# Attention of a hybrid decoder layer: the repetition of the inverse softmax denominators moves from VectorE to ScalarE

## The chip, the cores and the metric

The kernel runs on one core of one Trainium2 chip. The metric is the device time of one execution in microseconds. Three runs of the kernel before stand beside one execution that the hardware profiler recorded; the times of the profile count from the start of its span.

## What is computed

The reference is one step of a decoder layer for a prompt of 512 tokens and for 8 sample tokens that share the weights. Cut to what matters here:

```
z  = rms_norm(x) @ w_in            # q, k, v of 12 heads x 64; B, C, u of the short convolution
q, k = rope(rms_norm(heads))       # per head
m = max(s);  p = exp(s - m);  den = sum(p);  num = p @ v       # per dilated window (128,1), (512,4), (2048,16)
attn = sum(num_i * c_i) / sum(den_i * c_i)                     # the three windows merged
y  = B * conv3_causal(C * u)
h  = x + concat(rms_norm(attn), rms_norm(y)) @ w_out
out = h + top-2-of-8-experts(in the best of 4 groups, rms_norm(h))   # 32 gated MLPs of 1024 x 256
```

For the prompt, the kernel merges the three windows by adding the logarithm of how many windows hold a key to the score, so that one softmax per head does. The division by the denominator is what the change touches.

## The kernel before

The program is written by hand for each engine; each engine runs its own list in order and waits on semaphores. Stages: input projection and rotary norm (to about 178 us of the span), prompt attention with the short convolution between (178 to 254 us), output projection, routing and the choice of experts (254 to 341 us), and the 32 experts in 16 pairs, whose weights stream through three slots of `ring`.

The prompt's attention has 24 units, `pair_units`: query tile `qt` from 3 down to 0, and in each the six head pairs `hp`. A unit has n = (qt + 1) x 128 keys, so its width falls from 512 to 128 columns. The stage is a software pipeline over `p` from 0: each engine's list holds, in iteration p, a piece of several units.

- PE in iteration p: the scores of unit p (L816), the transposition of the exponentials of unit p - 1 (L933, into `turn_bank`), and for u = p - 2 the product of the probabilities with v (L949) and behind it one transposition of `rden_b` (L952), which raises `o_done`.
- DVE in iteration p: `masked_scores` of unit p (L1695: adds `logc`, keeps the minimum of the negated scores), for u = p - 1 the reciprocal of two denominators (L1759), the copy of the second head's transposed exponentials out of PSUM (L1760), and the repetition of the two inverses over 64 columns each into `rden_b` (L1762), which raises `p_evac_v`; then a piece of the convolution (`convolve`, p = 2 to 11); last, for u = p - 3, the product of the result in PSUM with the turned inverses (L1777, by the helper of L1521), which raises `o_evac`.
- ACT in iteration p: the exponentials of unit p for both heads (L1377, with the sum of the row by an accumulator read), for u = p - 3 the copy of the turned inverses out of PSUM into `rden_t` (L1384), for u = p - 1 the copy of the first head's transposed exponentials (L1394). In iteration 12 a square of the convolution's result follows (L1397), in iteration 16 the squares of the sample rows (L1402).
- POOL, once `w_out` has landed (210 us): for every unit one scaling of 512 columns of `w_out` (L2267, 16 times), and the square (L2273) and the running sum (L2274) of the attention's result.

A head's inverse denominator stands on the partition of its query, the result of L949 on the partition of its channel. So the inverse is repeated over 64 columns, turned by PE into a tile with the queries along the columns, and multiplied in. PE waits for `p_evac_v` ahead of L949 and for nothing ahead of L952.

## Time and profile before

| | |
|---|---|
| median of three runs | 596.61 us (594.55 to 598.19) |
| profiled execution, its own time | 592.48 us |
| its span | 590.7 us |
| PE, DVE, ACT, POOL busy | 545.4, 274.7, 167.9, 155.4 us |
| granted TensorE clock, mean | 0.983 |
| prompt attention on PE | about 178 to 254 us |

Busy time is the time in which an engine has an instruction in work. PE's matmuls overlap and their ends are modelled, so idle time of PE in a stretch is only what no modelled matmul covers. "idle before" of a group is the idle time of its engine just ahead of its instructions, with what ended it. DVE's L1521 is the line of a helper for products of two tensors; its tiles tell which one it is (`ring<-bank,ring` 128x128 is the product with the turned inverses, `work<-work,ring` 128x512 a product of the convolution).

### The profile page before, as it was taken

The page shows a single profiled execution, that of the slowest core. Times are in us where ns is not written, and L with a number is a line of the kernel's source. Part 1 is how long each engine was busy: PE and PEld are TensorE (multiplying, and loading weights), DVE is VectorE, ACT ScalarE, POOL GpSimd, SP SyncE. Part 2 cuts the span into 40 slices and gives each one's busy share as a digit, 9 for nine tenths or more (in the row PEclk, how much of TensorE's full clock was granted, in tenths as well). Part 3 has the DMA queues.
Part 4 walks back from the last instruction along what each step waited for, and adds up shares of the span by engine and source line. Part 5 has one row for each costly group of instructions (what it writes and reads, how often), then busy time and mean ns, then how long its engine had stood idle before and what let it go on. Part 6 is the DMA issues. An engine that isn't in the chain of part 4 may idle for free.

```text
span 590.7 us, 8412 instructions
## 1 busy us (share of the span) xinstructions
PE 545.4 (92%) x2970; PEld 318.3 (54%) x2970; DVE 274.7 (47%) x695; ACT 167.9 (28%) x386; POOL 155.4 (26%) x187
## 2 busy tenths in 40 slices
PE   6899999999999999999999999999996969689994
PEld 4798799897765665554555944333332323234321
DVE  5887686978403998723458631111210111111235
ACT  7445343413411566631412320101100100000013
POOL 0488788510001079610000021211210111100003
PEclk9999999999999999999999999999997979999998
DMA  7991333489774950039914869999999999999956
GB/s 280 281 272 51 123 134 94 152 249 301 238 196 150 381 208 2 3 95 383 413 41 173 327 194 414 418 421 420 421 420 422 421 419 421 419 422 418 378 235 260
DMA packets 48215, 163.48 MB, mean 277 GB/s; under 512 B 8674, under 2 KB 22058, under 8 KB 36888
## 3 DMA queue, kind: packets, MB, share of 16 engines
q1 hardware_dynamic: 41360, 144.93, 64.9%
q0 software_dynamic: 6528, 17.01, 8.1%
q10 hardware_dynamic: 288, 1.05, 0.4%
q8 instruction: 21, 0.34, 0.2%
q14 instruction: 18, 0.15, 0.1%
HBM read 151.06 MB, written 19.76 MB: 289 GB/s over the span
## 4 chain that ended last, share of the span: by engine, by line
PE 49%; DMA 17%; SPq 11%; DVE 5%; POOL 3%; issue 3%; ACT 2%; DVEq 0%; POOLq 0%; ACTq 0%
PE bank L1144 10%; DMA ring<-in_w_up_dram 10%; PE bank L1068 9%; SPq L540 7%; PE bank L1171 4%; DMA x<-q_rows 3%; SPq L553 3%; PE bank L816 2%; PE bank L933 2%; DMA ring<-results 2%; PE bank L949 2%; PE bank L838 2%; POOL ring L2225 2%; PE bank L1019 2%; PE bank L839 2%
## 5 line engine op out<-in xcount | busy, mean ns | idle before, releaser
L1144 PE MATMUL bank<-ring,work 128*64 128x512 f32 x512 | 120.1, 624 | 16.9 <-DMA ring<-in_w_up_dram 16.9
L1144 PEld LDWEIGHTS bank<-ring,work 128*64 128x64 f32 x512 | 39.1, 143 | 94.5 <-issue 80.5
L1521 DVE TENSOR_TENSOR work<-work,bank 128x256 f32<-128x256 f32 x16 | 6.7, 422 | 132.5 <-ACT work L1456 132.5
L759 PE MATMUL bank<-split 128*128 128x384 f32 x192 | 66.1, 344 | 0.7 <-DVE split L1521 0.7
L1171 PE MATMUL bank<-ring,work 128*64 128x512 f32 x256 | 58.5, 598 | 7.6 <-ACT work L1460 7.6
L760 PE MATMUL bank<-split 128*128 128x384 f32 x192 | 64.3, 335 | 0.0
L1068 PE MATMUL bank<-ring 128*128 128x512 f32 x96 | 42.9, 596 | 0.0
L1456 ACT ACTIVATE work<-bank 128x256 f32<-128x256 f32 x16 | 6.1, 384 | 128.5 <-PE bank L1144 128.5
L2292 POOL DMA_INDIRECT work<-hn_rows,tbl x15 | 15.2, 1016 | 101.7 <-PE bank L1154 89.7
L2300 POOL DMA_INDIRECT results<-work,tbl x15 | 15.0, 1001 | 99.1 <-DVE work L2070 99.1
L2225 POOL TENSOR_TENSOR ring<-ring 128x192 f32<-128x192 f32 (+1 forms) x40 | 38.8, 989 | 8.0 <-DVEq L1616 6.8
L1521 DVE TENSOR_TENSOR split<-ring,split 128x768 fp32r<-128x768 f32 (+1 forms) x35 | 37.3, 1099 | 6.1 <-PE bank L746 5.8
L790 PE MATMUL bank<-split 128*128 128x384 f32 x192 | 37.8, 337 | 0.5 <-DVE split L1521 0.5
L759 PEld LDWEIGHTS bank<-split 128*128 128x128 f32 x192 | 36.1, 188 | 3.5 <-issue 1.3
L1171 PEld LDWEIGHTS bank<-ring,work 128*64 128x64 f32 x256 | 17.0, 136 | 38.8 <-issue 27.4
L1377 ACT ACTIVATE ring<-ring,st 128x512 f32<-128x512 f32 (+3 forms) x48 | 26.6, 554 | 35.3 <-DVE st L1695 35.3
L760 PEld LDWEIGHTS bank<-split 128*128 128x128 f32 x192 | 36.1, 188 | 0.0
L2070 DVE COPY work<-bank 128x512 f32<-128x512 f32 x15 | 10.4, 692 | 52.8 <-PE bank L1171 52.8
L790 PEld LDWEIGHTS bank<-split 128*128 128x128 f32 x192 | 33.4, 188 | 1.7 <-DVE split L1521 1.0
L1068 PEld LDWEIGHTS bank<-ring 128*128 128x128 f32 x96 | 17.8, 190 | 20.1 <-issue 20.1
L1256 ACT ACTIVATE split<-ring 128x768 fp32r<-128x768 f32 x32 | 25.1, 833 | 3.8 <-DMA ring<-in_w_in_dram 3.8
L1469 ACT ACTIVATE work<-bank 128x512 f32<-128x512 f32 x15 | 9.0, 597 | 57.1 <-PE bank L1171 57.1
(281 smaller groups left out, 865.1 us busy)
## 6 DMA issues: line engine op xcount, KB each, us to landing
ring<-in_w_down_dram SPq DMA_DIRECT2D x32, 1024.0 KB, 24.7
ring<-in_w_gate_dram SPq DMA_DIRECT2D x28, 1024.0 KB, 23.1
ring<-in_w_up_dram SPq DMA_DIRECT2D x28, 1024.0 KB, 24.9
ring<-in_w_in_dram SPq DMA_DIRECT2D x7, 1536.0 KB, 11.7
results<-work POOLq DMA_DIRECT2D x1, 4160.0 KB, 24.7
x<-in_x_prompt_dram SPq DMA_DIRECT2D x8, 512.0 KB, 15.5
ring<-in_w_out_dram SPq DMA_DIRECT2D x2, 2048.0 KB
ring<-in_w_gate_dram SPq DMA_DIRECT2D x8, 512.0 KB, 13.2
```

The lines of the kernel that those rows point to most:

```text
L540: sp.dma_start(gate_up[s][h][:, o, :, :], w[0, ds(e, 1)].rearrange("e (p k) f -> p (e k) f", p=P)).then_inc(gu_in[s], 16)
L553: sp.dma_start(down[s][h], w_down[0, ds(e, 1)].rearrange("e (p k) n -> p (e k) n", p=P)).then_inc(dn_in[s], 16)
L759: pe.matmul(bank[n % 3][:, 0:CW], xT_high[:, k, cols], w_high[c][:, k, :], start=(k == 0), stop=False)
L760: pe.matmul(bank[n % 3][:, 0:CW], xT_low[:, k, cols], w_high[c][:, k, :], start=False, stop=False)
L790: last = pe.matmul(bank[n % 3][:, 0:CW], xT_high[:, k, cols], w_low[c][:, k, :], start=False, stop=(k == KD - 1))
L1068: last = pe.matmul(bank[g][:, :], src, wout[g % 2][:, k, :], start=(k == rng[0]), stop=(k == rng[-1]))
L1144: last = pe.matmul(bank[2][64 * h:64 * h + 64, :], xgT[:, k, 64 * h:64 * h + 64], gate_up[s][h][:, :, k, :], start=(k == 0), stop=(k == KD ...
L1171: last = pe.matmul(bank[4 + j][64 * h:64 * h + 64, :], hT[:, c, 64 * h:64 * h + 64], down[s][h][:, c, j * 512:(j + 1) * 512], start=(c == ...
L1256: act.activation(w_high[c][:, 2 * i:2 * i + 2, :], wchunk[c][:, 2 * i:2 * i + 2, :], ACT.Copy)\
L1377: act.activation(buf, buf, ACT.Exp, bias=nmax[:, u % 4:u % 4 + 1], scale=-1.0, accum_out=den[:, u % 24:u % 24 + 1]).then_inc(S["exp_done"], 1)
L1521: return dve.tensor_tensor(out, a, b, op)
L2225: last = pool.tensor_tensor(sv[:, :, a * half:(a + 1) * half], zv[:, :, b * half:(b + 1) * half], bc(rope_g[2 * (cc // 2) + 1][0:w, t, a * ...
```

## The change

DVE writes the two inverses and raises a new semaphore `inverted`; the copy of the exponentials behind it raises `p_evac_v`. ACT waits for `inverted` behind its own copy of the exponentials, repeats the two inverses over 64 columns into `rden_b`, and raises `rden_wide`. PE waits for `rden_wide` between L949 and the transposition of `rden_b`. Three semaphores that were each raised once (`gains_turned`, `a_turned`, `conv_turned`) become the three counts of one, `rows_turned`.

```diff
@@ PE
-            pe.transpose(bank[7][:, 0:30], ...).then_inc(S["gains_turned"], 1)
+            pe.transpose(bank[7][:, 0:30], ...).then_inc(S["rows_turned"], 1)
...
-                last.then_inc(S["conv_turned"], 1)
+                last.then_inc(S["rows_turned"], 1)
...
-                last.then_inc(S["a_turned"], 1)
+                last.then_inc(S["rows_turned"], 1)
...
                             pe.matmul(bank[6 + u % 2][h * DH:(h + 1) * DH, 0:P],
                                       v_rows[:, j, (2 * hp + h) * DH:(2 * hp + h + 1) * DH],
                                       probs_t[u % 2][h][:, j * P:(j + 1) * P], start=(j == 0), stop=(j == qt))
+                    pe.wait_ge(S["rden_wide"], u + 1)
                     pe.transpose(bank[6 + u % 2][:, P:2 * P], rden_b[:, u % 2, :, :].rearrange("p h d -> p (h d)"), ident[:, :])\
                         .then_inc(S["o_done"], 1)
@@ ACT
                     act.activation(probs_t[u % 2][0][:, 0:n], turn_bank[0][:, 0:n], ACT.Copy).then_inc(S["p_evac_a"], 1)
+                    act.wait_ge(S["inverted"], u + 1)
+                    act.activation(rden_b[:, u % 2, :, :], bc(rden[:, u % 2, :], 2, DH, [P, 2, DH]), ACT.Copy)\
+                        .then_inc(S["rden_wide"], 1)
                 if p == 12:
...
-            act.wait_ge(S["conv_turned"], 1)
+            act.wait_ge(S["rows_turned"], 3)
@@ DVE
                     if u >= 2:
                         dve.wait_ge(S["o_done"], u - 1)
-                    inverse = chain.put(dve.reciprocal(rden[:, u % 2, :], den[:, (2 * u) % 24:(2 * u) % 24 + 2]))
-                    dve.tensor_copy(probs_t[u % 2][1][:, 0:n], turn_bank[1][:, 0:n])
-                    chain.need(inverse)
-                    dve.tensor_copy(rden_b[:, u % 2, :, :], bc(rden[:, u % 2, :], 2, DH, [P, 2, DH])).then_inc(S["p_evac_v"], 1)
+                    dve.reciprocal(rden[:, u % 2, :], den[:, (2 * u) % 24:(2 * u) % 24 + 2]).then_inc(S["inverted"], 1)
+                    dve.tensor_copy(probs_t[u % 2][1][:, 0:n], turn_bank[1][:, 0:n]).then_inc(S["p_evac_v"], 1)
...
-                    dve.wait_ge(S["a_turned"], 1)
+                    dve.wait_ge(S["rows_turned"], 2)
```

How the lists stand at two places. The lines of the changed kernel count from its own text: L1385 is L1384 of before, L1395 is L1394, L1406 is L1402, L1378 is L1377, L1763, L1764 and L1525 are L1759, L1760 and L1521, and L1397 is the new copy on ACT.

ACT in iteration 16, where the squares of the sample rows stand; before:

```order
L1384 ACTIVATE ring<-bank 128x128 [waits o_evac,o_done]
L1394 ACTIVATE ring<-bank 128x256 [waits o_done,p_turned]
L1402 ACTIVATE work,st<-ring 8x768 [waits rows_out]
L1377 ACTIVATE ring,st<-ring,st 128x256 [waits masked] x2
L1384 ACTIVATE ring<-bank 128x128 [waits o_evac,o_done]
```

and with the change:

```order
L1385 ACTIVATE ring<-bank 128x128 [waits o_evac,o_done]
L1395 ACTIVATE ring<-bank 128x256 [waits o_done,p_turned]
L1397 ACTIVATE ring<-ring 128x128 [waits inverted]
L1406 ACTIVATE work,st<-ring 8x768 [waits rows_out]
L1378 ACTIVATE ring,st<-ring,st 128x256 [waits masked] x2
L1385 ACTIVATE ring<-bank 128x128 [waits o_evac,o_done]
```

The new copy stands behind the copy of the exponentials and ahead of the squares and of the next unit's exponentials; so it does in each of the 24 units.

DVE in iteration 10, where the last products of the convolution stand; before:

```order
L1759 RECIPROCAL ring<-st 128x2 [waits o_done,p_turned]
L1760 COPY ring<-bank 128x384
L1762 COPY ring<-ring 128x128 [waits dve_link]
L1521 TENSOR_TENSOR work<-work,ring 128x512
L1521 TENSOR_TENSOR ring<-bank,ring 128x128 [waits p_evac_a,o_done]
L1695 ISA ring,st<-bank,rt 128x384 [waits p_turned,s_done]
```

and with the change:

```order
L1763 RECIPROCAL ring<-st 128x2 [waits o_done,p_turned]
L1764 COPY ring<-bank 128x384
L1525 TENSOR_TENSOR work<-work,ring 128x512
L1525 TENSOR_TENSOR ring<-bank,ring 128x128 [waits p_evac_a,o_done]
L1699 ISA ring,st<-bank,rt 128x384 [waits p_turned,s_done]
```

The repetition is gone from between the copy of the exponentials and the products. (In iteration 8 the same piece of the list stands, for the other half of the channels.) On PE nothing changes place; the transposition L952, now L953, has a wait of its own.

## Rows read from the trace of the kernel before

**Rows 1.** The page: busy time of the engines, and the chain that ended last.

```profile
PE 545.4 (92%) x2970; PEld 318.3 (54%) x2970; DVE 274.7 (47%) x695; ACT 167.9 (28%) x386; POOL 155.4 (26%) x187
...
PE 49%; DMA 17%; SPq 11%; DVE 5%; POOL 3%; issue 3%; ACT 2%; DVEq 0%; POOLq 0%; ACTq 0%
```

**Rows 2.** Busy time by stretches: length, engines (instructions), granted clock, DMA share, GB/s.

```profile
188.00:220.00 32.00, 31.87 (x268) 19.41 (x262) 28.86 (x95) 18.43 (x53) 10.48 (x16) 1.00 0.85 319
220.00:236.00 16.00, 14.59 (x129) 9.14 (x125) 13.86 (x54) 11.14 (x40) 14.82 (x24) 1.00 0.01 3
236.00:254.00 18.00, 16.93 (x139) 8.97 (x139) 11.72 (x63) 11.89 (x53) 12.19 (x23) 1.00 0.01 2
254.00:330.00 76.00, 75.76 (x306) 41.49 (x305) 36.91 (x155) 20.87 (x33) 2.94 (x5) 1.00 0.64 241
```

**Rows 3.** Start of the experts' weights on SyncE, and a piece of the chain (start, length, what).

```profile
260.38 0.41 SPq L572 DMA_DIRECT2D ring<-in_w_gate_dram  x1
...
419.03 29.77 DMA ring<-in_w_up_dram
```

**Rows 4.** DVE's repetition as a group, and its shortest, median and longest.

```profile
L1762 DVE COPY ring<-ring 128x128 f32<-128x128 f32 x24 | 9.6, 401 | 0.0
...
L1762 DVE COPY ring<-ring x24: 210/220/1094, 191.8 to 251.3; 128x128 f32<-128x128 f32 x24
```

**Rows 5.** Timeline of iterations 10 and 11: DVE, POOL and PE (start, length).

```profile
220.43 1.09 DVE L1762 COPY ring<-ring 128x128 f32<-128x128 f32 x1
221.44 1.25 DVE L1521 TENSOR_TENSOR work<-work,ring 128x512 f32<-128x512 f32 x2
222.61 0.28 DVE L1521 TENSOR_TENSOR ring<-bank,ring 128x128 f32<-128x128 f32 x1
...
220.40 1.04 POOL L2267 TENSOR_TENSOR ring<-ring,gains 128x512 f32<-128x512 f32 x1
...
222.94 0.88 PE L949 MATMUL bank<-ring 128*64 128x128 f32 x12 [0.52 <-DVE ring L1521]
...
225.38 0.30 PE L933 MATMUL bank<-ident,ring 128*128 128x128 f32 x1 [0.67 <-ACT ring L1394]
```

**Rows 6.** Timeline of iteration 8: a product of the convolution beside POOL's sum.

```profile
215.31 0.68 DVE L1521 TENSOR_TENSOR work<-work,ring 128x512 f32<-128x512 f32 x1
215.91 0.28 DVE L1521 TENSOR_TENSOR ring<-bank,ring 128x128 f32<-128x128 f32 x1
...
215.38 0.92 POOL L2274 TENSOR_TENSOR ring<-ring 128x128 f32<-128x128 f32 x1
```

**Rows 7.** Timeline of ACT around iteration 12, with its square of 1040 columns.

```profile
227.79 1.06 ACT L1397 ACTIVATE ring<-work 128x1040 f32<-128x1040 f32 x1
228.75 0.50 ACT L1377 ACTIVATE ring<-ring,st 128x256 f32<-128x256 f32 x1
...
229.73 0.26 ACT L1384 ACTIVATE ring<-bank 128x128 f32<-128x128 f32 x1
229.89 0.38 ACT L1394 ACTIVATE ring<-bank 128x256 f32<-128x256 f32 x1
```

**Rows 8.** Timeline of ACT and PE around iterations 16 and 17.

```profile
236.56 0.83 ACT L1402 ACTIVATE work<-ring 8x768 f32<-8x768 f32 x1
...
239.09 0.63 PE L933 MATMUL bank<-ident,ring 128*128 128x128 f32 x4 [0.39 <-ACT ring L1394]
```

**Rows 9.** Timeline of one unit of 128 keys on ACT, and PE's transposition of the inverses.

```profile
243.98 0.26 ACT L1394 ACTIVATE ring<-bank 128x128 f32<-128x128 f32 x1
...
244.71 0.40 ACT L1377 ACTIVATE ring<-ring,st 128x128 f32<-128x128 f32 x1 [0.47 <-DVE st L1695]
...
245.11 0.33 PE L952 MATMUL bank<-ident,ring 128*128 128x128 f32 x1
```

**Rows 10.** Groups of ACT in the stage, shapes apart: exponentials, 128 and 256 columns.

```profile
L1377 ACT ACTIVATE ring<-ring,st 128x256 f32<-128x256 f32 x12 | 6.0, 501 | 2.8 <-DVE st L1695 2.8
...
L1377 ACT ACTIVATE ring<-ring,st 128x128 f32<-128x128 f32 x12 | 4.7, 393 | 3.1 <-DVE st L1695 3.1
```

More of the change, by code:

```diff
@@ L302, in build @@
         names = """const_in gains_in misc_in x_evac_p wr_in wout_in logc_in
-            row_std x_scaled x_turned x_whole x_high x_evac w_high_done w_low_done gains_turned rope_ready pads_zero
+            row_std x_scaled x_turned x_whole x_high x_evac w_high_done w_low_done rows_turned rope_ready pads_zero
             z_done z_squared z_ssq z_std z_copied z_normed z_cos z_sin z_summed rot_turned rot_evac v_evac rows_out
-            part_done part_evac comb_done comb_read gates_turned gates_read blk_done blk_evac_a blk_evac_v cu_ready conv_done y_squared pool_made ssc_done
-            ssc_std conv_std state_turned conv_turned conv_evac conv_out
+            part_done part_evac comb_done comb_read gates_turned gates_read blk_done blk_evac_a blk_evac_v cu_ready conv_done y_squared inverted rden_wide pool_made ssc_done
+            ssc_std conv_std state_turned conv_evac conv_out
             q_out scores_s turned_s soft_in soft_done probs_turned probs_placed v_used pv_s head_done
@@ L309, in build @@
             s_done masked exp_done p_turned p_evac_a p_evac_v o_done o_evac
-            a_squared a_std a_turned a_evac opp_done op_done op_evac opp_evac h_done
+            a_squared a_std a_evac opp_done op_done op_evac opp_evac h_done
             h_root h_scaled h_turned h_evac r_done r_evac
@@ L644, in _ @@
             pe.wait_ge(S["gains_in"], 80)
-            pe.transpose(bank[7][:, 0:30], gain_in[0:30, :], ident[0:30, 0:30]).then_inc(S["gains_turned"], 1)
+            pe.transpose(bank[7][:, 0:30], gain_in[0:30, :], ident[0:30, 0:30]).then_inc(S["rows_turned"], 1)
             def keep_warm(n, where):
@@ L1528, in _ @@
             dve.wait_ge(S["pads_zero"], 1)
-            dve.wait_ge(S["gains_turned"], 1)
+            dve.wait_ge(S["rows_turned"], 1)
             chain.step(dve.tensor_copy(gains[:, 0:30], bank[7][:, 0:30]))
```

## The prediction

> **What bounds the kernel now.** I read the page first for who bounds the whole [rows 1]: PE is busy for 92% of the span and holds 49% of the chain that ended last; DVE is busy for 47% and holds 5%. So an edit on DVE or ACT pays only where PE stands idle for it. Then the stretches [rows 2] for the stage that the change touches. In 188 to 220 us PE is busy 31.87 of 32.00 us, in 220 to 236 us 14.59 of 16.00, in 236 to 254 us 16.93 of 18.00. The idle time of PE is 0.13 + 1.41 + 1.07 = 2.61 us, and that is all that shorter work on the other engines can win here by these rows, 0.44% of the run. The clock is granted in full (1.00) in all of them. DVE is busy 28.86 of 32.00 us in the first stretch, nearly as much as PE, and 13.86 of 16.00 in the second; ACT 18.43, 11.14 and 11.89.
>
> What is won or lost there reaches the end. From 254 to 330 us PE is busy again 75.76 of 76.00 us [rows 2], and the first load of experts' weights is issued at 260.38 us [rows 3], when PE has closed the stage (SyncE waits for `ssc_done` ahead of it). The chain turns to the weights' transfers much later, at 419.03 us [rows 3], in a stream whose starts the same PE list has set. So I count a shift of the stage as the same shift of the end.
>
> Last the groups and the timeline of the repetition itself. L1762 runs 24 times for 9.6 us, 401 ns on average, but the median is 220 and the longest 1094 [rows 4]. The timeline shows where the long ones come from [rows 5]: the repetition at 220.43 starts 0.03 us behind POOL's scaling L2267 (220.40, 1.04 long) and ends when that has ended. Behind it two products of the convolution follow at 221.44, the product of unit 7 at 222.61, and PE's L949 waits 0.52 us for that product; through the minimum and the exponentials that follow on DVE and ACT, L933 then waits 0.67 us at 225.38. These two gaps, 1.19 us, are the part of the 2.61 us that the repetition can be blamed for.
>
> **The change part by part.** The 24 repetitions leave DVE: 9.6 us of its busy time [rows 4]. DVE holds 5% of the chain [rows 1], so most of it is worth nothing: PE was busy beside it.
>
> First place, iterations 10 to 12 [rows 5]. With the repetition gone, the convolution's products are next on DVE, and can start at 220.43. From their start to the product of unit 7 it took 222.61 - 221.44 = 1.17 us. Undisturbed by POOL's scaling the product would come at 220.43 + 1.17 = 221.60, 1.01 us sooner, and the two gaps would close by as much. But at 220.43 the scaling still runs to 221.44, and whether it holds a product as it held the repetition these rows don't show. If it does, the products start to move at 221.44, as before, and nothing is won. In iteration 8 a large product ran beside POOL's sum [rows 6] in 0.68 us with 0.60 to the next instruction, and the sum took 0.92 us: so the two kinds do get in each other's way, and there the product came first. The term lies between 0 and -1.01 us. I take -0.4, nearer to the held case, because here POOL comes first. The Trainium skill, SBUF — State Buffer, section Who interferes with whom, says that a VectorE instruction with two SBUF inputs contends with a GpSimd instruction that reads SBUF, and that the first to issue holds the shared ports for its whole length. By that rule this term would be near 0 instead of -1.01; the sum drawn out to 0.92 us agrees with it [rows 6], and no row shows a product held by the scaling.
>
> Second place, the convolution's iterations before 210 us, where DVE runs back to back. Each repetition takes 0.22 us there [rows 4]; PE's idle time in the whole stretch is 0.13 us [rows 2], so the term is 0 to -0.13 us; I take -0.1.
>
> The repetitions arrive on ACT. No row of before shows an ACT copy of 128 columns from SBUF. The nearest from below is the copy of 128 columns from PSUM, which gives way to the next instruction after 0.16 us [rows 7] (229.73 to 229.89); from above an exponential of 128 columns from SBUF, 0.393 us [rows 10]. The square of 1040 columns from SBUF gave way after 0.96 us [rows 7], that is 0.00088 us more for each column beyond 128 than the PSUM copy, so source and function weigh little, and I take 0.20 us. In most units that is covered: ACT stands idle ahead of the exponentials, waiting for DVE's minimum, and the shortest of these waits is where units are narrow, 0.47 us at 244.71 [rows 9]; the copy needs 0.20 of it, at most 0.39. If that cover were gone, all 24 copies would be on the path, 4.8 us.
>
> Two units have no such wait. In iteration 12 the square runs from 227.79 to 228.75 and the exponential follows at once; the copies at 229.73 and 229.89, on which PE's L933 waits, would come 0.20 us later [rows 7]. In iteration 16 the squares of the sample rows start at 236.56 behind the copy of the exponentials [rows 8]; the new copy goes between, and PE, which already waits 0.39 us at 239.09 for ACT, waits 0.20 longer. Together +0.4 us, 0 to 0.78 by the bounds.
>
> PE gets a wait ahead of L952. In a narrow unit ACT's copy of the exponentials starts at 243.98 and takes 0.26 us; the repetition behind it would be done by about 244.24 + 0.39 = 244.63 even at the upper bound, and PE comes to L952 at 245.11 [rows 9]. It costs nothing; behind it on PE would stand the next scores. DVE raises `inverted` before it copies the exponentials, and ACT comes to it after its own copy, so ACT's new wait is covered too: what is queued behind it, the next exponentials, needs a later result of DVE anyway. `p_evac_v` comes earlier by the repetition, which PE, busy, can't use. The merged semaphores move nothing.
>
> The Trainium skill, Perfetto Trace Analysis, section Optimizing Scalar/DVE Operations, speaks against the change: what both engines can do is faster on VectorE where a performance mode is open to it, and should move when VectorE is saturated. Here the median of 0.22 us against my 0.20 doesn't bear out a loss by length, and DVE at 13.86 of 16.00 us is not the bound; by that rule the sum would be the +0.4 us of the two units alone (the second rival).
>
> **Sum:** -0.4 - 0.1 + 0.4 = -0.1 us. The profiled execution took 592.48 us, so 592.4; it lies 4.1 us under the median of the three runs. On the median of 596.61 that gives **596.5 us**.
>
> **The rivals.** *All of PE's waiting goes.* The products run free, the narrow units lose their waits too: 2.61 us at most, 594.0 us. For it: the two largest gaps hang on the repetition [rows 5]. Against it: the rest, as the 0.39 us at iteration 17, ends on ACT [rows 8], where work is added. The likelier part of it is -1.14 us, 595.5.
>
> *Nothing is won on DVE.* The products stand in the repetition's place in DVE's list and wait for POOL's scaling in its stead: from 221.44 on all is as before, the first two terms are 0, and the two late copies on ACT stay: +0.4 us, 597.0. For it: the scaling starts 0.03 us ahead of them [rows 5]. Against it: in iteration 8 the product, not POOL, had its way [rows 6], and a shift of DVE by a tenth of a microsecond against POOL decides who is first. The rule on shared ports named above is this rival's.
>
> *The hold moves along to ACT.* If POOL's scaling holds a copy on ACT as it held DVE's, some five of the 24 repetitions take up to 1.09 us, as the longest on DVE [rows 4], and ACT is late with the next exponentials by 1.09 - 0.47 = 0.62 us each [rows 9], 3.1 us in all: 599.7, slower. It decides from the point where the copy takes longer than ACT's wait, 0.47 us. Against it: exponentials of 256 columns ran 12 times at a mean of 501 ns [rows 10] in the very stretch in which POOL is busy 14.82 of 16.00 us [rows 2], so ACT's traffic with SBUF is not held. The same would follow, with 4.8 us and 601.4, if no copy were covered.
>
> *The change does not reach the end.* The experts' weights stream at their own pace from 419 us on [rows 3]; a microsecond sooner or later at 254 us could vanish in it: 596.6.
>
> **How the numbers follow.** My forecast 0.49, all or most of PE's waiting goes 0.18, nothing won on DVE 0.20, the hold on ACT 0.07, no effect at the end 0.06. Run to run, the kernel before spread from 594.55 to 598.19, 2.06 below and 1.58 above its median; about 0.5%, 3.0 us, is what a measurement can tell from no change. The bounds of my terms are -1.01 - 0.13 = -1.14 and +0.78; with the spread they reach from 593.4 to 599.0. Cut to hold 8 of 10, the range is 593.8 to 598.6. Faster by over 0.5% would need more than all of PE's idle time, 0.04; slower by over 0.5% is the hold on ACT, 0.07; within 0.5% is the rest, 0.89.
>
> **What would show it.** Right: DVE's busy time falls by about 9 us and ACT's grows by 24 x 0.3, near 7; the new copy on ACT has one length throughout; PE's L953 waits for nobody; PE's idle time from 188 to 254 us stays between 1.4 and 3.4 us; the waits at iterations 13 and 17 grow by 0.2 us, the pair of 0.52 and 0.67 shrinks. Wrong: copies of over 0.47 us on ACT, a PE wait that ends on the repetition, a product of the convolution that starts right behind the copy of the exponentials and lets PE run through, or a change of 3 us or more.

## The result, and the profile after

The changed kernel takes 592.82 us (median of 9 runs, 590.96 to 594.61), the kernel before beside it 597.08 us (9 runs, 594.55 to 598.31): ratio 0.994, 95% interval 0.9913 to 0.9968. It is faster by 0.3 to 0.9%. Three more comparisons of 12 runs each against 35 of the kernel before gave 0.9969 (0.9938 to 0.9999), 0.9942 (0.9914 to 0.9970) and 0.9962 (0.9925 to 0.9999); the kernel before against itself gave 1.0011 (0.9983 to 1.0040) and 1.0003 (0.9975 to 1.0031). One execution of the changed kernel in these comparisons, 628.66 us long at a mean granted clock of 0.847, was in a slow state and is left out. So the gain is there, about 0.45%. I had forecast 596.5 us, a gain of 0.1.

The profiled execution of the changed kernel shows none of it: 592.82 us with a span of 591.1, where that of the kernel before took 592.48 with 590.7. These are the lines of its page that answer to [rows 1]: busy time by engine, and the chain that ended last.

```profile
PE 544.0 (92%) x2970; PEld 318.1 (54%) x2970; DVE 269.2 (46%) x671; ACT 172.8 (29%) x410; POOL 155.7 (26%) x187
...
PE 58%; DMA 13%; SPq 11%; DVE 3%; issue 2%; ACT 2%; POOL 1%; DVEq 0%; POOLq 0%; ACTq 0%
```

DVE lost 24 instructions and 5.5 us, ACT gained 24 instructions and 4.9 us; both are less than the groups' own sums, 9.6 [rows 4] and 24 x 0.30 = 7.2 us, because neighbours on an engine overlap by about 0.1 us and the overlap counts once, and on DVE also because other instructions became longer. PE's share of the chain, 49% before and 58% here, says nothing of the change: it is 57% in another profile of the kernel before, and 58, 50, 48 and 58% in the four of the changed one. The stretches of the changed kernel that answer to [rows 2], with the same columns:

```profile
188.00:220.00 32.00, 31.50 (x265) 19.01 (x258) 27.65 (x81) 19.75 (x61) 11.60 (x17) 1.00 0.85 320
220.00:236.00 16.00, 15.78 (x139) 9.91 (x136) 12.21 (x52) 13.46 (x50) 14.90 (x23) 1.00 0.01 3
236.00:254.00 18.00, 16.70 (x142) 9.13 (x140) 8.78 (x55) 13.30 (x59) 11.54 (x23) 1.00 0.01 2
254.00:330.00 76.00, 75.76 (x306) 41.45 (x305) 37.40 (x159) 21.00 (x31) 3.48 (x5) 1.00 0.65 249
```

PE's idle time is now 0.50 + 0.22 + 1.30 = 2.02 us instead of 2.61. It vanished in the middle stretch, 1.41 to 0.22, and grew in the other two. These are PE's waits in 188 to 254 us of the changed kernel (the bracket: us waited, and for what):

```profile
211.62 1.09 PE L949 MATMUL bank<-ring 128*64 128x128 f32 x16 [0.21 <-DVE ring L1525]
214.06 0.85 PE L933 MATMUL bank<-ident,ring 128*128 128x128 f32 x6 [0.24 <-ACT ring L1395]
238.56 0.63 PE L933 MATMUL bank<-ident,ring 128*128 128x128 f32 x4 [0.52 <-ACT ring L1395]
243.84 0.42 PE L933 MATMUL bank<-ident,ring 128*128 128x128 f32 x2 [0.20 <-ACT ring L1395]
...
```

Of the pair of 0.52 and 0.67 us at 222.94 and 225.38 [rows 5] 0.12 us is left, ahead of L933 at 224.87, too short for these lines to name. In its place stands a smaller pair at 211.62 and 214.06, where PE waits for nobody in the kernel before. The wait of 0.39 us at iteration 17 [rows 8] is 0.52. The timeline of the changed kernel at iterations 10 and 11, answering to [rows 5], DVE first, then POOL:

```profile
220.60 0.54 DVE L1764 COPY ring<-bank 128x384 f32<-128x384 f32 x1
221.05 1.03 DVE L1525 TENSOR_TENSOR work<-work,ring 128x512 f32<-128x512 f32 x2
222.01 0.28 DVE L1525 TENSOR_TENSOR ring<-bank,ring 128x128 f32<-128x128 f32 x1
...
219.58 1.04 POOL L2269 TENSOR_TENSOR ring<-ring,gains 128x512 f32<-128x512 f32 x1
220.58 0.40 POOL L2275 TENSOR_TENSOR ring<-ring 128x128 f32<-128x128 f32 x1
221.06 0.99 POOL L2276 TENSOR_TENSOR ring<-ring 128x128 f32<-128x128 f32 x1
```

The convolution's products start right behind the copy of the exponentials, and 0.01 us later POOL's sum L2276 starts and is drawn out to 0.99 us (0.45 where nothing holds it): this time POOL is the one that is held. The scaling that had held the repetition lies earlier, at 219.58, because POOL's whole list starts earlier. Its first scaling waits for the output weights; the row of the kernel before, then that of the changed kernel, from POOL's timelines:

```profile
210.27 1.20 POOL L2267 TENSOR_TENSOR ring<-ring,gains 128x512 f32<-128x512 f32 x1 [20.59 <-DMA ring<-in_w_out_dram]
```

```profile
209.29 1.03 POOL L2269 TENSOR_TENSOR ring<-ring,gains 128x512 f32<-128x512 f32 x1 [19.40 <-DMA ring<-in_w_out_dram]
```

The new copy on ACT, as the trace lists that line (shortest, median, longest in ns; first and last start):

```profile
L1397 ACT ACTIVATE ring<-ring x24: 291/300/310, 192.8 to 251.1; 128x128 f32<-128x128 f32 x24
```

It has one length throughout, and PE's L953 waits for nobody.

Attention, from PE's first scores (L816) to the first transposition of the convolution's rows (L891), is 75.28 us long, before 76.04: 0.76 us shorter. PE's idle time gives 0.59 us of that; the rest lies where the modelled matmuls cover the waiting. In the traces of the three repeats it is 75.19, 75.36 and 75.44; in two repeats of the kernel before 76.04 and 76.05. So 0.60 to 0.85 us can be seen, 0.10 to 0.14% of the run, a quarter to a third of what the clocks outside the trace show. The experiments had two questions: does the seen part come of DVE's relief, and where is the rest?

### The profile page after: what moved, and what is told of

The parts are those of the page before. It is cut to its first block, busy times and chain, and to the rows that moved or that the text cites. A ratio compares the mean times of both kernels' runs of the same rounds, so it can differ in the third digit from the quotient of the medians.

```text
span 591.1 us, 8412 instructions
## 1 busy us (share of the span) xinstructions
PE 544.0 (92%) x2970; PEld 318.1 (54%) x2970; DVE 269.2 (46%) x671; ACT 172.8 (29%) x410; POOL 155.7 (26%) x187
## 2 busy tenths in 40 slices
DMA packets 48215, 163.48 MB, mean 277 GB/s; under 512 B 8674, under 2 KB 22058, under 8 KB 36888
## 4 chain that ended last, share of the span: by engine, by line
PE 58%; DMA 13%; SPq 11%; DVE 3%; issue 2%; ACT 2%; POOL 1%; DVEq 0%; POOLq 0%; ACTq 0%
PE bank L1145 10%; DMA ring<-in_w_up_dram 10%; PE bank L1069 9%; SPq L540 8%; PE bank L1172 4%; PE bank L790 4%; PE bank L759 3%; PE bank L760 3%; SPq L553 3%; PE bank L933 3%; PE bank L816 2%; DMA ring<-results 2%; PE bank L949 2%; PE bank L838 2%; PE bank L1020 2%
## 5 line engine op out<-in xcount | busy, mean ns | idle before, releaser
L1525 DVE TENSOR_TENSOR work<-work,bank 128x256 f32<-128x256 f32 x16 | 6.7, 421 | 132.5 <-ACT work L1460 132.5
L1525 DVE TENSOR_TENSOR split<-ring,split 128x768 fp32r<-128x768 f32 (+1 forms) x35 | 37.3, 1099 | 6.2 <-PE bank L746 5.9
L1378 ACT ACTIVATE ring<-ring,st 128x512 f32<-128x512 f32 (+3 forms) x48 | 26.5, 554 | 30.1 <-DVE st L1699 30.1
```

Of the source, the lines that this page charges most:

```text
L1378: act.activation(buf, buf, ACT.Exp, bias=nmax[:, u % 4:u % 4 + 1], scale=-1.0, accum_out=den[:, u % 24:u % 24 + 1]).then_inc(S["exp_done"], 1)
L1525: return dve.tensor_tensor(out, a, b, op)
```

## The experiments

Each kernel was run 12 times. "Attention" is the length just defined, in the one profiled execution of that kernel; PE's busy time in it is 73.1 to 73.4 us. What each theory says stands in the expectation.

**The two kernels again.**

> The kernel before, unchanged, against itself: what the comparison gives for nothing, and a second look at the attention. If attention varies from run to run (the hold of VectorE's repetition behind POOL falls differently each time), its profile has PE idle for clearly more or less than 2.61 us between 188 and 254 us; if the profiled execution of before was typical of the stage, it is again 2.4 to 2.8 us and the time is within 0.3% of before.

> The changed kernel again, beside the others on one chip. If the 0.6% is the change's, the ratio is 0.991 to 0.997 again. If it came from which chip or hour the runs fell on, it is 0.997 to 1.003, as the two traces say (attention 0.75 us shorter, 0.1%).

> The changed kernel a third time, to fix the size. Theory one (only attention is shorter, by the 0.75 to 0.85 us of two traces, and the rest of the 0.6% first measured is how many runs happened to have the early fall of the clock near 331 to 361 us): over all runs 0.997 to 0.9995, and runs of like mean clock differ from before by 0.5 to 1.5 us. Theory two (the change itself makes the early fall rarer): ratio 0.991 to 0.996 and clearly fewer runs of mean clock under 0.978 than before has.

> The changed kernel a fourth time, as the third: theory one 0.997 to 0.9995, theory two 0.991 to 0.996 with few runs of mean clock under 0.978.

> The kernel before against itself once more, on the chip of the other three: 0.998 to 1.002 if the comparison is as even as its interval says; attention 76.0 us with PE idle 2.6 us.

The ratios stand above. The second profile of the changed kernel shows the same products of iteration 10 in another order against POOL, DVE first:

```profile
220.20 1.61 DVE L1525 TENSOR_TENSOR work<-work,ring 128x512 f32<-128x512 f32 x2
221.73 0.28 DVE L1525 TENSOR_TENSOR ring<-bank,ring 128x128 f32<-128x128 f32 x1
...
220.33 1.44 POOL L2269 TENSOR_TENSOR ring<-ring,gains 128x512 f32<-128x512 f32 x1
```

Now the first product starts 0.13 us ahead of the scaling, which is drawn out from 1.04 to 1.44 us, and the second product pays: the two take 1.61 us instead of 1.03. So which engine is held depends on who started first, and that differs from run to run with POOL's first scaling, which waits for the output weights (it starts at 208.43, 209.29, 209.65 and 210.38 us in the four executions of the changed kernel). Within some hundredths of a microsecond the recorded starts don't decide it: at 211.83 us of this profile a product of 8 columns on DVE starts 0.02 us ahead of a scaling and still takes 1.08 us, 0.22 where nothing holds it. The step that the prediction left open, whether the scaling holds a product as it held the repetition, is answered here: it does. The Trainium skill, SBUF — State Buffer, section Who interferes with whom, has this rule (a VectorE instruction with two SBUF inputs contends with a GpSimd instruction that reads SBUF); these rows agree with it.

**Without the repetition.** Before, with the inverses written once:

```diff
...
-                    dve.tensor_copy(rden_b[:, u % 2, :, :], bc(rden[:, u % 2, :], ...)).then_inc(S["p_evac_v"], 1)
...
+                    if u < 2:
+                        dve.memset(rden_b[:, u % 2, :, :], 0.01)
+                    dve.tensor_copy(probs_t[u % 2][1][:, 0:n], turn_bank[1][:, 0:n]).then_inc(S["p_evac_v"], 1)
```

> The repetition is left out altogether: rden_b holds a constant written in the first two units, so attention is scaled by a constant in place of the denominators. Theory one (VectorE's repetition, held behind POOL, is what costs): as fast as the changed kernel or up to 0.4 us faster, since ACT is spared the two late copies of iterations 12 and 16. Theory two (the gain comes from somewhere else, such as the earlier p_evac_v or the clock and the weights' stream later): slower than the changed kernel by 2 us or more.

And the changed kernel with ACT's copy under `if u < 2`, and PE's wait at most for the second:

> The changed kernel without the repetition from the third unit on (rden_b keeps the first two units' values, so later units are divided by the wrong denominators); waits and semaphores as in the changed kernel. Attention about 74.9 us, as when the repetition was left out of the kernel before. Theory one: 0.2 to 0.4 us faster than the changed kernel in attention, and a ratio against before within 0.002 of what leaving it out gave there (1.0001). Theory two: 0.994 to 0.9965, clearly faster than that.

Attention 74.93 and 75.65 us, ratios 1.0001 (0.9969 to 1.0033) and 0.9986 (0.9952 to 1.0019). The second was to have 74.9 us. The first has the shortest attention of all, 1.1 us shorter than before, and no gain. Its profile shows where that is given back. PE's wait for the weights of the seventh pair of experts, first in the changed kernel, then in this one:

```profile
430.77 5.80 PE L1145 MATMUL bank<-ring,work 128*64 128x512 f32 x26 [0.29 <-DMA ring<-in_w_up_dram]
```

```profile
431.60 4.94 PE L1144 MATMUL bank<-ring,work 128*64 128x512 f32 x22 [1.73 <-DMA ring<-in_w_up_dram]
```

But these kernels cannot be compared behind attention. Their attention has other values, and what follows depends on them: every kernel with the true inverses moves 8674 packets under 512 B (one shows 8675), those with constant ones 8676 or 8677, so what follows attention is not the same. That the 1.4 us of extra wait comes of that is not shown: the kernel before with a pause, further down, has the true inverses and waits 1.28 us for the same weights. I use these two for attention's length alone.

**The repetition as a reduction on DVE.**

```diff
-                    dve.tensor_copy(rden_b[:, u % 2, :, :], bc(rden[:, u % 2, :], ...)).then_inc(S["p_evac_v"], 1)
+                    dve.tensor_reduce(rden_b[:, u % 2, :, :], bc(rden[:, u % 2, :], ...).unsqueeze(3), AX.X, ALU.add)\
+                        .then_inc(S["p_evac_v"], 1)
```

> The repetition stays on VectorE but as a sum over an axis of one element, 128 columns from SBUF to SBUF. If a copy is held behind POOL because of its form and a reduction is not, no repetition takes over 0.35 us, and the time falls by what the hold cost (0.5 to 1.2 us in attention by the traces). If the reduction is held as well, the longest is again near 1.1 us and the time is that of before.

The trace of that line, which answers to [rows 4]:

```profile
L1762 DVE TENSOR_REDUCE ring<-ring x24: 270/276/279, 192.7 to 252.0; 128x128 f32<-128x128 f32 x24
```

The reduction is never held, where the copy ran up to 1.09 us. Yet attention is 75.95 us and the ratio 1.0014 (0.9981 to 1.0047). PE waits 0.42, 0.24 and 0.36 us at 212.68, 215.12 and 220.95. The first two do not come of the reduction: the kernel before with the semaphores merged, below, in which POOL starts at nearly the same point of attention (31.9 us from its start, here 32.0), waits 0.43 and 0.24 us there too, and its third wait, 0.42 us, stands later, at 226.04. The third wait here follows from a product of the convolution that is held, behind which ACT waits 1.58 us for the minimum (to 218.96):

```profile
216.54 0.28 DVE L1762 TENSOR_REDUCE ring<-ring 128x128 f32<-128x128 f32 x1
216.74 1.52 DVE L1521 TENSOR_TENSOR work<-work,ring 128x512 f32<-128x512 f32 x1
...
216.66 1.04 POOL L2268 TENSOR_TENSOR ring<-ring,gains 128x512 f32<-128x512 f32 x1
```

The scaling starts 0.07 us ahead of the product, which takes 1.52 us (0.68 us where it came first). That is the case of the forecast, and it is the held one. Freeing one instruction from POOL was worth nothing here, as DVE had as much to do and the next instruction was caught in its place.

**The squares of the sample rows earlier**, at iteration 4 instead of 16, in the changed kernel:

```diff
-                if p == 16:
+                if p == 4:
                     act.wait_ge(S["rows_out"], 48)
```

> The changed kernel with the squares of the sample rows on ACT moved from iteration 16 to iteration 4, where ACT waits more than 1 us for VectorE. If the wait at iteration 17 (0.49 us behind PE's scores) is ACT's squares plus the new copy, it shrinks to 0.1 to 0.2 us and attention takes 74.8 to 74.95 us instead of 75.2 to 75.3; the time follows by 0.3 us, less than the comparison can show. If something else holds iteration 17, attention stays at 75.2.

PE's wait at iteration 17, 0.52 us in the changed kernel, is here

```profile
238.62 0.63 PE L933 MATMUL bank<-ident,ring 128*128 128x128 f32 x4 [0.17 <-ACT ring L1395]
```

so what grew there was ACT's queue, as predicted. Attention did not shorten: 75.39 us, with a wait of 0.40 us at 225.29 and one of 0.40 at 211.76. The ratio is 0.9984 (0.9951 to 1.0016).

**ACT's copy twice in each unit**, the first of the two into a spare tile:

```diff
+                    act.activation(rden_x[:, u % 2, :, :], bc(rden[:, u % 2, :], ...), ACT.Copy)
```

> The changed kernel with ACT's copy done twice in every unit (the second time into a spare tile). If ACT's wait for the minimum covers a copy of 0.2 us twice over (0.47 us in the narrow units), attention grows by 0.2 to 0.6 us only, at iterations 13 and 17. If the copies are on the path, it grows by 24 x 0.2 = 4.8 us.

Both copies as groups (count, busy us, mean ns, idle before):

```profile
L1398 ACT ACTIVATE ring<-ring 128x128 f32<-128x128 f32 x24 | 7.2, 302 | 0.0
L1399 ACT ACTIVATE ring<-ring 128x128 f32<-128x128 f32 x24 | 7.2, 299 | 0.0
```

Another 7.2 us of work on ACT left attention at 75.32 us and the ratio at 0.9968 (0.9935 to 1.0000). PE's wait at iteration 17 grew by one copy, from 0.52 to 0.72 us; everywhere else ACT's wait for the minimum covers the copies.

**The merged semaphores alone**, in the kernel before:

```diff
-                last.then_inc(S["conv_turned"], 1)
+                last.then_inc(S["rows_turned"], 1)
...
-            act.wait_ge(S["conv_turned"], 1)
+            act.wait_ge(S["rows_turned"], 3)
```

> The kernel before with the semaphores alone as the change has them (three merged into one, two new ones declared and not used); every instruction and wait stays where it was. Theory one (the change gains by its shorter attention, 0.6 to 0.85 us, and the rest of the measured 0.4 to 0.6% is how the falls of the clock and the weights' stream happened to come out): attention 76.0 us and a ratio of 0.998 to 1.002. Theory two (something that goes with the new text as such, not with attention): 0.996 to 0.9975.

Attention 75.98 us, ratio 1.0000 (0.9973 to 1.0027): nothing.

**PE held up at the end of attention**: dummy products `keep_warm(n, bank[2])` ahead of the transposition of the convolution's rows.

> The changed kernel with eight more matmuls of 128 columns on PE between the last unit's transposition and the conv rows, 8 x 0.109 = 0.87 us, so that PE leaves attention when it did before. Theory one: the gain is gone, ratio 0.998 to 1.002, and the first load of experts' weights is issued at 260.3 us or later. Theory two: it keeps more than half, 0.994 to 0.9975.

The pause was 1.79 us, twice what I had put down, and the ratio 1.0005 (0.9977 to 1.0032) with attention at 76.93. So with three products in place of eight, in both kernels:

> The changed kernel with three dummy products on PE between attention and the transposition of the convolution's squares: by the trace of the longer pause (8 products, 16 entries, 1.79 us) that is 0.67 us, so attention is about 76.0 us long, as in the kernel before. Theory one (all that the change gives runs through the time at which PE leaves attention): as the kernel before, 0.999 to 1.001. Theory two (about a microsecond of the gain is made elsewhere, by ACT's copies or by what lies behind them): still 1.1 to 1.3 us faster than before, 0.998. Theory three (what is not accounted for comes of how PE's arrival meets the stream of weights behind pair 6, where PE waited 0.29 us in the changed kernel and 1.73 us in the kernel without the repetition): as before, and the wait behind pair 6 decides, 0 to 1.9 us.

> The kernel before with the same three dummy products, 0.67 us, at the same place: attention about 76.7 us. Theories one and three: 0.7 us slower, 1.001. If the weights' stream sets the end and takes the delay up: 1.000. Theory two says the same as theory one. It is the measure of what 0.67 us of PE's time at that place is worth at the end.

The changed kernel with the pause of 0.67 us: attention 75.95 us, as long as in the kernel before, and the ratio 0.9950 (0.9923 to 0.9976). The kernel before with it: attention 77.22 us, ratio 1.0035 (1.0003 to 1.0067). In the kernel before, PE's time at this place reaches the end, then (the same pause in the changed kernel cost nothing that can be told); and a gain is left when attention is as long as before. **The attention that the trace shows isn't all of it.**

**ACT's copies without relief for DVE**, and without PE's dependence. In the first, the changed kernel's ACT copies go to a spare tile and DVE repeats as before; in the second, only the inverses of the first two units are written and the 22 later copies on ACT go to a spare tile:

> DVE makes the repetition as in the kernel before (behind its copy of the exponentials), and ACT makes the same copies as in the changed kernel, into a spare tile that nobody reads; PE waits for DVE alone, as before. Theory one: attention 76.0 us or up to 0.2 us longer, 1.000. Theory two (the copies on ACT themselves, by what they do to the order of events later, bring what attention's length does not explain): 1.1 us faster, 0.998. Theory three: 1.000, with the wait behind pair 6 as the spread.

> The changed kernel with the repetition written only in the first two units, for later units PE reads those (attention's output is then scaled by wrong inverses), and with ACT's copies of the later units kept, into a spare tile. Beside the run without those 22 copies (0.9986) it differs by them alone, beside the changed kernel by PE's dependence alone. Theory one: attention 75.2 to 75.6 us, 0.9985 to 0.9990. Theory two: as the changed kernel, 0.9965. Theory three: between the two, with the wait behind pair 6 as in the changed kernel (near 0.3 us) if the copies set it, or near 1.6 us if not.

Ratios 1.0003 (0.9971 to 1.0035) and 0.9995 (0.9966 to 1.0024), attention 76.34 and 75.14 us. ACT's copies by themselves bring nothing. The second is one of the kernels with other values, and has the longest wait of all for the seventh pair, 1.89 us; it tells nothing of the rest.

**DVE's load alone, and the signals alone.** The changed kernel with the repetition put back on DVE behind the signal, into a spare tile; and the changed kernel with the repetition on DVE alone, ACT's removed, the signals kept:

```diff
                     dve.tensor_copy(probs_t[u % 2][1][:, 0:n], turn_bank[1][:, 0:n]).then_inc(S["p_evac_v"], 1)
+                    dve.wait_ge(S["inverted"], u + 1)
+                    dve.tensor_copy(rden_x[:, u % 2, :, :], bc(rden[:, u % 2, :], ...))
```

> The changed kernel with DVE's repetition put back beside ACT's, behind its copy of the exponentials and behind the signal to PE, into a spare tile that nobody reads: DVE's load is that of the kernel before (24 copies of 0.22 to 1.09 us), what PE waits for is that of the changed kernel. If the gain is made by DVE's load (the minimum and the convolution's products coming sooner, as the trace of attention shows it): as the kernel before, 0.999 to 1.001, PE idle about 2.6 us in attention. If it is made elsewhere: still near 1.9 us faster, 0.9965 to 0.998, though the trace of attention is 76.0 us long.

> The changed kernel with the repetition on DVE alone, behind the copy of the exponentials, and with the changed kernel's signals: PE gets the copy of the exponentials announced ahead of the repetition, and waits for the repetition by itself ahead of the transposition of the inverses. ACT has nothing to do with it. If the gain is made by DVE's load: as before, 1.000. If it is made by the earlier announcement of the exponentials or by PE's separate wait: near 1.9 us faster, 0.9965 to 0.998. If ACT's copies are needed for it: as before too, and the run with both copies tells that case apart from the first.

Ratios 1.0012 (0.9980 to 1.0044) and 1.0000 (0.9964 to 1.0036); attention 76.24 and 75.59 us. **With the repetition back on DVE no gain is left that can be told** (the intervals leave room for 0.2 and 0.36%), though in the first nobody reads what it writes and every wait and signal of the changed kernel is kept; DVE only waits for its own inverses in addition. Attention of the second is 0.45 us shorter than before although DVE makes all repetitions, so not all of the shortening that traces show can be put down to DVE's relief; the signals may bring it, or POOL, which in that profile starts 33.1 us after attention's start, in the three of the kernel before at 32.2 to 32.4. The trace of the first, its repetition and PE's waits:

```profile
L1767 DVE COPY ring<-ring x24: 215/217/1039, 192.3 to 251.9; 128x128 f32<-128x128 f32 x24
```

```profile
212.16 1.09 PE L950 MATMUL bank<-ring 128*64 128x128 f32 x16 [0.42 <-DVE ring L1526]
...
225.71 0.85 PE L934 MATMUL bank<-ident,ring 128*128 128x128 f32 x6 [0.41 <-ACT ring L1396]
230.93 0.63 PE L934 MATMUL bank<-ident,ring 128*128 128x128 f32 x4 [0.25 <-ACT ring L1396]
239.69 0.63 PE L934 MATMUL bank<-ident,ring 128*128 128x128 f32 x4 [0.52 <-ACT ring L1396]
...
```

The waits are those of the changed kernel again, longer, and one more, at 230.93. It is ended by ACT, but the delay is DVE's: the repetition at 224.62 is held for 1.04 us, and ACT then waits 0.82 us for the minimum behind it, 0.39 us in the changed kernel.

**Side by side**, the kernels that compute with the true inverses:

| kernel | repetitions that DVE makes | attention, us | ratio |
|---|---|---|---|
| before, three profiles | 24 | 76.04, 76.04, 76.05 | 1.0011, 1.0003 |
| semaphores merged | 24 | 75.98 | 1.0000 |
| as a reduction | 24 | 75.95 | 1.0014 |
| DVE and ACT both, PE on DVE's | 24 | 76.34 | 1.0003 |
| DVE and ACT both, PE on ACT's | 24 | 76.24 | 1.0012 |
| on DVE, new signals | 24 | 75.59 | 1.0000 |
| before, pause 0.67 | 24 | 77.22 | 1.0035 |
| changed, four profiles | 0 | 75.28, 75.19, 75.36, 75.44 | 0.9940, 0.9969, 0.9942, 0.9962 |
| changed, squares earlier | 0 | 75.39 | 0.9984 |
| changed, ACT twice | 0 | 75.32 | 0.9968 |
| changed, pause 0.67 | 0 | 75.95 | 0.9950 |
| changed, pause 1.79 | 0 | 76.93 | 1.0005 |

All but one of the rows without DVE's repetitions lie at 0.9940 to 0.9984, all rows with them at 1.0000 or above, and the exception holds a pause as long as the gain. The squares earlier, 0.9984, are no weaker case: only one of their 12 runs has a mean granted clock of 0.98 or more, and the other 11 take 595.4 us where the kernel before beside them takes 597.7 below that clock; ACT twice has 595.5 (8 runs). The kernels with DVE's load alone and the signals alone take 596.3 (7 runs) and 596.5 us (6 runs) below that clock, against 596.8 before. Among these kernels DVE's relief is what the change is worth; the three with other values, which have the relief and no gain, are left out of that. What the table does not give is the place of the part beyond attention's 0.6 to 0.85 us.

## Why the prediction was wrong

**Two steps failed: the sum's third term, +0.4 us for the two late copies on ACT, measured next to nothing; and "I count a shift of the stage as the same shift of the end" held only for a part of the gain: attention became 0.60 to 0.85 us shorter, the run about 1.9 us at an equal mean clock, and where the rest is made stays open.** The terms can be read off the transposition of the inverses on PE, in units 4, 10 and 16, before and then changed:

```profile
209.34 0.33 PE L952 MATMUL bank<-ident,ring 128*128 128x128 f32 x1
...
226.96 0.33 PE L952 MATMUL bank<-ident,ring 128*128 128x128 f32 x1
...
240.23 0.33 PE L952 MATMUL bank<-ident,ring 128*128 128x128 f32 x1
```

```profile
209.43 0.33 PE L953 MATMUL bank<-ident,ring 128*128 128x128 f32 x1
...
226.45 0.33 PE L953 MATMUL bank<-ident,ring 128*128 128x128 f32 x1
...
239.70 0.33 PE L953 MATMUL bank<-ident,ring 128*128 128x128 f32 x1
```

Attention starts at 177.92 us before and at 178.13 here. So the changed kernel gains 0.13 us up to unit 4, 0.60 from there to unit 10, 0.02 from there to unit 16, and nothing behind. In its other three profiles it gains 0.13 each time up to unit 4, then 0.68, 0.52 and 0.44, then 0.01 to 0.02. The second term, -0.1, was right.

The first term was "I take -0.4, nearer to the held case, because here POOL comes first"; it was worth -0.44 to -0.68 us, a little more. PE's two waits at iterations 10 and 11, 1.19 us [rows 5], are 0.12, 0.61, 0.12 and 0.78 us in the four profiles of the changed kernel; where they are 0.12, the new pair at iterations 7 and 8 takes 0.45 and 0.53. The mechanism was right, in both of its cases: POOL's scaling holds a product when it comes first, and is held when it comes second. What I missed is that nothing fixes who comes first. POOL's start hangs on a transfer, and moved by up to 1.95 us from run to run; two of the four profiles have the one pattern and two the other, and a hold that goes from one place can come up at another. That the term came near its value is in part luck.

The third term, +0.4 us, came out at -0.01 to -0.02. At iteration 17 the wait grew by 0.13 us instead of 0.20 [rows 8]. At iteration 13 no wait grew. ACT at iteration 12 in the changed kernel, answering to [rows 7]:

```profile
226.83 0.30 ACT L1397 ACTIVATE ring<-ring 128x128 f32<-128x128 f32 x1
227.03 1.06 ACT L1401 ACTIVATE ring<-work 128x1040 f32<-128x1040 f32 x1
227.99 0.50 ACT L1378 ACTIVATE ring<-ring,st 128x256 f32<-128x256 f32 x1
```

The copy delays the square by 0.20 us, as I had it. But I had looked at one held repetition only, and in the kernel before the next one, in iteration 11, is held as long; ACT waits 1.02 us for the minimum behind it, 0.39 us in the changed kernel:

```profile
224.29 1.04 DVE L1762 COPY ring<-ring 128x128 f32<-128x128 f32 x1
...
226.26 0.51 ACT L1377 ACTIVATE ring<-ring,st 128x256 f32<-128x256 f32 x1 [1.02 <-DVE st L1695]
```

```profile
225.31 0.51 ACT L1378 ACTIVATE ring<-ring,st 128x256 f32<-128x256 f32 x1 [0.39 <-DVE st L1699]
```

Counted from attention's start, ACT comes to the square 0.97 us earlier than before, copy included, and PE to unit 10 0.73 us earlier: ACT is not late there. By the attention that the traces show the sum should have been -0.60 to -0.85 us, not -0.1, about 595.9 us on the median. That is still no change by my own bound, and the range from 593.8 would have held it. The rest of the error is the part of the gain that these traces don't show. Nor was PE's idle time of 2.61 us "all that shorter work on the other engines can win here": of attention's gain, 0.16 to 0.28 us in each profile is no idle time of PE by the modelled ends.

**What came true.** The copy has one length, 0.30 us, and gives way after 0.20; L953 waits for nobody; PE's idle time, 2.02 us, lies between 1.4 and 3.4; the pair of 0.52 and 0.67 us shrank, here to 0.12. Of the signs of being wrong, two came: a product of the convolution right behind the copy of the exponentials that lets PE run on, at 221.05 us, and a change of over 3 us in the first comparison. The rivals of the hold moving to ACT (no copy over 0.310 us) and of nothing won on DVE are out; *All of PE's waiting goes*, 594.0 us, is nearest to what was measured, though in the traces 2.0 of the 2.61 us remain. *The change does not reach the end* is out by the gain itself. ACT's busy time grew by 4.9 us and not 7, and DVE's fell by 5.5 and not 9, as overlaps count once; DVE's also because the time that POOL takes from DVE does not leave with the instruction that was held: a copy of 16 columns, L1743, is now held to 0.91 us (0.38 before).

**What stays open.** Between the runs the time spreads by 5 us and more, and the cause of the largest part shows in the traces: in some executions the granted clock falls near 333 and 358 us, in a stretch where PE does not wait. The same two stretches of the changed kernel in its first profile, then in its second (columns as in [rows 2]):

```profile
325.00:340.00 15.00, 15.00 (x131) 14.70 (x131) 10.15 (x55) 4.47 (x5) 0.95 (x1) 1.00 0.74 292
355.00:365.00 10.00, 9.52 (x51) 3.96 (x52) 1.78 (x4) 0.77 (x2) 1.50 (x2) 1.00 1.02 413
```

```profile
325.00:340.00 15.00, 15.00 (x103) 14.70 (x103) 9.00 (x54) 4.45 (x5) 0.95 (x1) 0.77 0.76 286
355.00:365.00 10.00, 10.00 (x50) 4.63 (x48) 0.85 (x2) 0.60 (x1) 1.01 (x1) 0.83 1.02 399
```

In the second the clock is 0.50, the level of 1.2 GHz, from 332 to 338 us; from 325 to 340 us PE is busy 15.00 us in both. From the end of attention to the first pair's down projection the first takes 96.1 us, the second 99.4. In every trace with no fall there, of whichever kernel, this length is 96.1 us, so the rest of the gain is not made in it. Nor is the gain a luckier share of such runs. Divide all runs by the mean clock granted over the run: at 0.98 and above the kernel before took 593.6 us (67 runs of 186), the changed kernel 591.9 (18 of 44); below that 597.1 and 595.0. The shares, 36 and 41%, differ little, and the gain is 1.8 and 2.1 us within either group. In the profiled executions without the two falls it is smaller: 592.48 and 592.43 against 592.82 and 592.22 us, no gain that can be told. So of about 1.9 us some 0.6 to 0.85 are seen in attention, and some 1.1 have no place in any trace. Behind the first pair the traces differ by about 1 us among runs of one kernel (240.6 to 241.6 us to the end in the changed one without falls), so a difference there can't be told from them. PE's 2.61 us of idle time would have room for it, if the holds between DVE and POOL were longer or more frequent in the executions that were not traced; that is an argument, and no trace here shows it. Nor is it settled whether DVE's relief acts by its time or by its 24 instructions fewer: every kernel with the repetitions back has both.

## What to carry to other kernels

Where two engines hold each other up, don't cost a freed instruction by the order that the one trace shows: list who starts within some tenths of a microsecond of whom, ask what sets either start (here a transfer whose landing moved by 1.95 us from run to run), and give both cases a real weight. Before a term for later work is added, ask whether its engine will still be late there once the change has freed what it waits for. Here less work on the engine that is held paid, and making one instruction immune did not: the reduction was never held and won nothing, the copies' removal won 0.45%. Behind a stage whose values steer later work, a kernel that leaves something out may be read only up to the end of that stage.

## What the runs showed of the hardware

- A copy of 128 columns on ACT from SBUF took 0.291 to 0.310 us in 24 of 24 cases, also in the stretch in which POOL was busy 14.90 of 16.00 us, and gave way to the next instruction after 0.20 us (226.83 to 227.03). On DVE the same copy took 0.22 us when free and up to 1.09 when POOL had started 0.03 us earlier, the reduction 0.270 to 0.279.
- The hold goes either way: POOL's scaling of 512 columns took 1.03 us alone and 1.44 beside a product that had started 0.13 us before it; its sum 0.45 alone and 0.99 behind a product 0.01 us ahead. A product of 512 columns on DVE took 0.68 us where it came first and 1.52 behind a scaling 0.07 us ahead.
- A satisfied wait costs PE nothing that the rows show: in a narrow unit the transposition of the inverses starts 0.37 us behind L949 in the kernel before (244.74 to 245.11) and in the changed one (244.20 to 244.57), where the new wait stands between them.
- The granted clock fell in some executions and not in others of the same kernel: in one profile of the changed kernel to 0.50 (1.2 GHz) from 332 to 338 us, in another not at all, with PE busy 15.00 of 15.00 us from 325 to 340 us in both. It cost 3.3 us (99.4 against 96.1 from the end of attention to the first pair's down projection).
